# Half of the one-hot gate products of a PEER layer replaced by additions in device memory

## The reference

```python
q = (ht @ w_q).reshape(T, PEER_HEADS, 2, D_HALF)
s1, s2 = einsum(q[:, :, 0], k1), einsum(q[:, :, 1], k2)       # T x 8 x 128 each
v1, i1 = lax.top_k(s1, 16);  v2, i2 = lax.top_k(s2, 16)
sc, flat = lax.top_k(v1[..., :, None] + v2[..., None, :], 16)  # of 256 sums
idx = e1 * 128 + e2;  gate = softmax(sc)
act = gelu(einsum('td,thkd->thk', x, u_tab[idx]))
out = einsum('thk,thkd->td', gate * act, v_tab[idx])
```

## Time and profile before

| | |
|---|---|
| median of 3 runs (lowest to highest) | 1903.39 us (1902.47 to 1903.56) |
| the profiled execution's own time | 1903.38 us |
| span of its instructions | 1901.6 us |
| granted TensorE clock, mean | 0.99 |
| up stages (tiles, scores, scatter) | 200 to 600 us and 1113 to 1512 us |
| down stages | 601 to 975 us and 1514 to 1890 us |

### The profile page before, as it was taken

The page is one execution under the profiler, slowest core; times in us unless marked ns, Lnnn a source line. Parts: engine busy times, 40 slices in busy tenths (PEclk is TensorE's granted clock), DMA queues, the critical chain, the costliest instruction groups (busy, mean ns, idle before and its releaser), DMA issues.

```text
span 1901.6 us, 39850 instructions
## 1 busy us (share of the span) xinstructions
PE 1860.2 (98%) x14863; PEld 1726.2 (91%) x14863; DVE 1524.4 (80%) x2634; ACT 858.2 (45%) x1281; POOL 4.0 (0%) x8
## 2 busy tenths in 40 slices
PE   5999999999999999999999999999999999999998
PEld 5999999999999888888889999999999988888887
DVE  7986689888888888888868768889788888885555
ACT  3335444454434444455444544444434444445453
POOL 0000000000000000000000000000000000000000
PEclk9999999999999999999988999999999999999999
DMA  7976455555444555688834745555544455555552
GB/s 301 335 277 236 154 179 185 177 176 170 153 166 139 171 176 167 235 325 319 321 127 168 262 158 177 179 185 185 168 146 165 138 172 165 176 187 190 197 189 99
DMA packets 101344, 370.46 MB, mean 195 GB/s; under 512 B 11168, under 2 KB 11552, under 8 KB 100640
## 3 DMA queue, kind: packets, MB, share of 16 engines
q1 hardware_dynamic: 100848, 367.43, 55.5%
q10 hardware_dynamic: 432, 2.23, 0.3%
HBM read 366.47 MB, written 3.15 MB: 194 GB/s over the span
## 4 chain that ended last, share of the span: by engine, by line
PE 91%; DVE 5%; DMA 2%; issue 1%; ACT 1%; SPq 0%; DVEq 0%; ACTq 0%
PE ps L1156 46%; PE acc L1315 36%; PE gp L1267 5%; DVE acts L591 2%; DVE low L572 2%; PE ps L1135 1%; PE gp L1077 1%; DMA raw<-conv_in 1%; PE gp L1256 1%; DMA acts<-w_mod 1%; PE gp L1099 0%; ACT high L371 0%; DMA raw<-conv_out 0%; PE acc L1094 0%; DVE acts L952 0%
## 5 line engine op out<-in xcount | busy, mean ns | idle before, releaser
L572 DVE TENSOR_TENSOR low<-raw,high 128x1024 fp32r<-128x1024 f32 x596 | 727.7, 1222 | 320.6 <-ACT high L371 318.5
L371 ACT ACTIVATE high<-raw 128x1024 fp32r<-128x1024 f32 x593 | 626.7, 1057 | 483.0 <-PE acc L1315 383.3
L1156 PE MATMUL ps<-mov_h,high 128*128 128x256 f32 x2656 | 761.2, 287 | 9.9 <-DVE mov_l L680 5.4
L1156 PE MATMUL ps<-mov_l,high 128*128 128x256 f32 x2656 | 755.4, 284 | 0.0
L1156 PE MATMUL ps<-mov_h,low 128*128 128x256 f32 x2656 | 755.2, 284 | 0.0
L1156 PEld LDWEIGHTS ps<-mov_h,high 128*128 128x128 f32 x2656 | 513.4, 193 | 11.5 <-issue 8.2
L1156 PEld LDWEIGHTS ps<-mov_l,high 128*128 128x128 f32 x2656 | 513.7, 193 | 0.0
L1156 PEld LDWEIGHTS ps<-mov_h,low 128*128 128x128 f32 x2656 | 513.6, 193 | 0.0
L1315 PE MATMUL acc<-high,mov_h 128*128 128x512 f32 x1024 | 402.6, 393 | 1.0 <-DVE mov_l L1009 0.8
L1315 PE MATMUL acc<-high,mov_l 128*128 128x512 f32 x1024 | 399.0, 390 | 0.0
L1315 PE MATMUL acc<-low,mov_h 128*128 128x512 f32 x1024 | 398.6, 389 | 0.0
(11 more groups left out here) (116 smaller groups left out, 802.4 us busy)
## 6 DMA issues: line engine op xcount, KB each, us to landing
raw<-up SPq DMA_DIRECT2D x256, 512.0 KB, 3.2
raw<-down SPq DMA_DIRECT2D x256, 512.0 KB, 4.0
acts<-w_mod SPq DMA_DIRECT2D x84, 512.0 KB, 5.8
raw<-query SPq DMA_DIRECT2D x32, 512.0 KB, 3.9
raw<-conv_in SPq DMA_DIRECT2D x24, 512.0 KB, 6.8
acts<-w_mod SPq DMA_DIRECT2D x6, 1024.0 KB, 14.7
raw<-conv_out SPq DMA_DIRECT2D x8, 512.0 KB, 7.0
raw<-pool_in SPq DMA_DIRECT2D x8, 512.0 KB, 3.9
```

The lines of the kernel that those rows point to most:

```text
L371: nc.scalar.activation(flat(high[s]), tile_row(s), ACT.Copy).then_inc(high_ready, 1)
L572: nc.vector.tensor_tensor(flat(low[n % RING]), tile_row(n % RING), flat(high[n % RING]).bitcast(F32), ALU.subtract).then_inc(low_ready, 1)
L1156: ins = nc.tensor.matmul(dst, w[s][:, c], m[:, mv], start=(first and n == 0), stop=(last and n == 2), skip_group_check=skip)
```

## The change

Tokens 0 to 127 get their dense gates in another way; tokens 128 to 255 keep the one-hot products, so that a half of the tiles now has 16 sets (pairs behind every sixth `up` tile from tile 83, and behind every eighth of the first 64 `down` tiles).

- A table of 128 x 128 x 128 float32 in device memory for each layer (8.4 MB) is cleared by SP with 16 transfers of 512 KB: layer 0's beside the query tiles and the first 8 `up` tiles of layer 0, layer 1's beside `up` tiles 8 to 39 of layer 0. Their source is `hot2`, filled with zeros.
- In each of the 8 rounds of `retrieval` DVE now finishes the round: softmax, expert number and place in the table (`DEST`). ACT's Exp comes 8 times in a layer, each followed by a load of the Gelu table.
- GpSimd's `add_gates` issues 16 indirect transfers for a round, each of which adds 128 single numbers (one for each token) to the table. A round's transfers wait until those of the round before have landed.
- GpSimd's `fetch` reads the table back, two tiles' gates of 128 tokens at a time (128 KB), into a ring of four buffers. The first is `added`, the other three are places 4 to 7 of `mov_h`, which are free once PE has done the last `up` tile. DVE's `weigh_first` multiplies tiles 2q and 2q + 1 of `A` by them, and ACT's `weight` waits for it.
- PE turns three blocks in place of six, behind tile 79 in place of tile 77.

```diff
-SETS = HALF // 2
-SET = T // SETS
+SET = 8
+SETS = P // SET
+CHUNK = 1024
+CHUNKS = KEYS * P // CHUNK
+WRING = 4
+WTILES = 2
+GROUPS = KEYS // WTILES
...
+        wt = [added[:]] + [mov_h[:, RING + n].bitcast(F32) for n in range(WRING - 1)]
...
+            def clear(layer, at):
+                cols = bass.ds(at, CHUNK) if not isinstance(at, int) else slice(at, at + CHUNK)
+                sp.dma_start(rows[layer][:, cols], nothing).then_inc(zeroed[layer], 16)
...
+            def add_gates(layer, p):
+                pool.wait_ge(picked, layer * HEADS + p + 1)
+                if layer or p:
+                    pool.wait_ge(landed, 16 * TOPK * (layer * HEADS + p))
+                for k in range(TOPK):
+                    col = p * TOPK + k
+                    nc.gpsimd.indirect_dma_start(
+                        table[layer], bass.IndirectOffsetOnAxis(ap=DEST[:, col:col + 1], axis=0),
+                        GT0[:, col:col + 1], None, compute_op=ALU.add).then_inc(landed, 16)
+            def fetch(layer, i, s, free):
+                if free is not None:
+                    pool.wait_ge(weighed, free)
...
+                nc.gpsimd.dma_start(wt[s], rows[layer][:, cols]).then_inc(wt_in[s], 16)
+            for layer in range(LAYERS):
+                pool.wait_ge(zeroed[layer], 16 * CHUNKS)
+                for p in range(HEADS):
+                    add_gates(layer, p)
+                pool.wait_ge(landed, 16 * TOPK * HEADS * (layer + 1))
+                for s in range(WRING):
+                    if s == 1:
+                        pool.wait_ge(product, AT[layer, "down"] + RING)
+                    fetch(layer, 0, s, layer * GROUPS - WRING + s + 1 if layer else None)
...
-                gelus(8, (TURN - RING - 8) // RING)
-                for s in range(RING):
-                    if s == 2:
-                        act.wait_ge(soft_in, layer + 1)
-                        nc.scalar.activation(SC, SC, ACT.Exp).then_inc(soft_exp, 1)
+                exps = {(HEADS + 1) * p + 11: p for p in range(HEADS)}
+                for j in range(8, TURN + 2 * HEADS):
+                    if j in exps:
...
+                        nc.scalar.activation(sc, sc, ACT.Exp).then_inc(soft_exp, 1)
                         load_table(ACT.Gelu)
...
+                    act.wait_ge(weighed, group + (layer * GROUPS + 1))
...
-                a = a[:, :, k * SET:(k + 1) * SET]
+                a = a[:, :, P + k * SET:P + (k + 1) * SET]
...
+            def weigh_first(layer, q):
+                dve.wait_ge(wt_in[q % WRING], 16 * (layer * (GROUPS // WRING) + q // WRING + 1))
+                a = A[:, WTILES * q * T:WTILES * (q + 1) * T].rearrange("p (g t) -> p g t", t=T)[:, :, 0:P]
+                nc.vector.tensor_tensor(a, a, wt[q % WRING].rearrange("p (g t) -> p g t", t=P),
+                                        ALU.mult).then_inc(weighed, 1)
...
-                    if (j - FIRST_SET) % 3 == 2:
+                    if (j - FIRST_SET) % 6 == 4:
                         two_sets(0, k)
                         k += 2
+                weigh_first(layer, 0)
...
                 for g in range(AHEAD):
+                    if g == WTILES:
+                        weigh_first(layer, 1)
                     low_weight(g)
...
-                    if j % 4 == 2:
-                        two_sets(1, j // 4 * 2)
+                    if j + 2 < GROUPS:
+                        weigh_first(layer, j + 2)
+                    if j % 8 == 2:
+                        two_sets(1, j // 8 * 2)
...
-                        if s % 3 == 1:
-                            scatter(0, i, s // 3 * 2, 8)
-                            scatter(0, i, s // 3 * 2 + 1, 8)
+                        if s % 6 == 3:
+                            scatter(0, i, s // 6 * 2, 4)
+                            scatter(0, i, s // 6 * 2 + 1, 4)
```

More of the change, by code:

```diff
@@ L169, in program @@
         EX = part(o + 1088, 2 * T)
-        GT = part(o + 1600, T)
+        GT1 = part(o + 1600, P)
+        PLACE = part(o + 1600 + P, TOPK)
         SUM = part(o + 1856, ROWS)
         RS = part(o + 1872, ROWS)
-        twice = hot2[:, 0, 0]
+        twice = part(15616, KEYS).bitcast(BF16).rearrange("p (n two) -> p n two", two=2)
+        nothing = hot2[:].rearrange("p a b c d -> p (a b c d)").bitcast(F32)
+        own = part(15616 + KEYS, P)
         v16 = part(o + 1888, 4 * TOPK).rearrange("p (r s n) -> p r s n", r=2, s=2)
@@ L214, in program @@
         soft_in, soft_exp = sem("soft_in"), sem("soft_exp")
+        picked, landed, weighed = sem("picked"), sem("landed"), sem("weighed")
+        zeroed = [sem(f"zeroed{n}") for n in range(LAYERS)]
+        wt_in = [sem(f"wt_in{n}") for n in range(WRING)]
         pick_done, turned, turned_out = sem("pick_done"), sem("turned"), sem("turned_out")
@@ L316, in _ @@
                                      ).then_inc(gate2_in[k], 16)
-                run(layer, "up", KEYS)
+                    elif layer == 0:
+                        clear(0, j // 2 * CHUNK)
+                if layer == 0:
+                    for j in range(8):
+                        load(0, "up", j, j % RING)
+                        clear(0, (8 + j) * CHUNK)
+                    with sp.Fori(0, CHUNKS // 2) as i:
+                        for s in range(RING):
+                            load(0, "up", i * RING + (8 + s), s)
+                            if s % 2:
+                                clear(1, i * (2 * CHUNK) + s // 2 * CHUNK)
+                    run(0, "up", KEYS - 8 - CHUNKS // 2 * RING, 8 + CHUNKS // 2 * RING)
+                else:
+                    run(1, "up", KEYS)
                 run(layer, "down", HALF)
@@ L361, in _ @@
             nc.gpsimd.memset(macc[:, 2:MODS].rearrange("p m n -> p (m n)"), 0.0).then_inc(const_ready, 1)
+            nc.gpsimd.memset(nothing, 0.0).then_inc(const_ready, 1)
+            def add_gates(layer, p):
[10 more added lines that the diff above has]
+                    pool.wait_ge(weighed, free)
+                n = WTILES * P
+                at = i * (WRING * n) + s * n
+                cols = bass.ds(at, n) if not isinstance(at, int) else slice(at, at + n)
+                nc.gpsimd.dma_start(wt[s], rows[layer][:, cols]).then_inc(wt_in[s], 16)
[8 more added lines that the diff above has]
+                    fetch(layer, 0, s, layer * GROUPS - WRING + s + 1 if layer else None)
+                with pool.Fori(0, GROUPS // WRING - 1) as i:
+                    for s in range(WRING):
+                        fetch(layer, i + 1, s, i * WRING + (layer * GROUPS + s + 1))
         @block.scalar
@@ L828, in retrieval @@
                     found = did(ins)
+                    need(top)
+                    need(found)
+                    sc = turn(SC, TOPK)[:, 2 * p:2 * p + 2]
+                    nc.vector.tensor_tensor(sc, sc, RS[:, 2 * p:2 * p + 2].unsqueeze(2).broadcast_to([P, 2, TOPK]),
+                                            ALU.subtract).then_inc(soft_in, 1)
+                    for _ in before:
+                        pass
                     beside()
-                    need(found)
                     before = numbers(p)
[L833 to L838, removed]
                 for _ in before:
                     beside()
[L841 to L847, removed]
+                dve.wait_ge(picked, HEADS * (layer + 1))
+                dve.sem_inc(pick_done, 1)
+                while tile[0] < FIRST_SET:
                     beside()
                 dve.wait_ge(turned, layer + 1)
-                nc.vector.tensor_copy(idx1[:], gp[:, 0, 0:T]).then_inc(turned_out, 1)
-                nc.vector.tensor_copy(idx2[:], gp[:, 0, T:2 * T]).then_inc(turned_out, 1)
-                full = gp[:, 1, 0:T].rearrange("p (h two) -> p h two", two=2)
+                if layer == 0:
+                    for n in range(LAYERS):
+                        dve.wait_ge(zeroed[n], 16 * CHUNKS)
+                nc.vector.tensor_copy(idx1[:], gp[:, 0, 0:P]).then_inc(turned_out, 1)
+                nc.vector.tensor_copy(idx2[:], gp[:, 0, P:2 * P]).then_inc(turned_out, 1)
+                full = gp[:, 1, 0:P].rearrange("p (h two) -> p h two", two=2)
                 rest = gate_rest.rearrange("p (h two) -> p h two", two=2)
@@ L1319, in down_banks, with arrived, down_tile @@
                         return ins
[L1321 to L1327, removed]
+                    def arrived(i, s, per=RING):
+                        pe.wait_ge(low_ready, i * per + (n0 + half * HALF + s + 1))
+                        pe.wait_ge(wl_ready, i * per + (layer * KEYS + half * HALF + s + 1))
+                    def down_tile(i, s, per=RING):
+                        arrived(i, s, per)
+                        down_banks(s % RING, range(4), False).then_inc(product, 1)
                     if half == 0:
-                        with pe.Fori(0, HALF // RING) as i:
-                            for s in range(RING):
-                                down_tile(i, s)
```

(3 more changed lines are left out.)

86 lines of the change are left out of this document (57 added, 29 removed).

## The result

| | before | changed |
|---|---|---|
| median of 4 runs (lowest to highest) | 1902.93 us (1902.19 to 1903.56) | 1853.05 us (1850.83 to 1854.15) |
| the profiled execution, own time | 1903.38 us | 1854.15 us |
| span | 1901.6 us | 1852.5 us |

The ratio is 0.9737 (95% interval 0.972 to 0.9753). The change takes off 49.9 us; I had forecast 44.9. The direction was right and PE's time went where I had said; the largest term of the sum, what a pair of sets costs, was too small.

The account below looks back on a forecast made before the run. PE, busy 98% of the span, was taken as the bound, with the sets' products hidden under nothing: 1903.4 - 47.0 - 0.7 + 2.8 = 1858.5 us. Likeliest case 1854 to 1871 us; range of 8 in 10, 1853 to 1896 us.

Parts of the forecast that it names:

- the products (47.0 us): PE, up and down stages: 32 of 64 pairs of one-hot sets go at 1.47 us each, 47.0 us less.
- Taken away: The PE work that goes: half of the 3072 one-hot products, 47.0 us, and three transposes a layer, 0.7 us.
- a pair's price is not what goes away: Sign that the forecast is wrong: removing a pair of sets does not save its 1.47 us.
- The transposes (0.7 us): PE: three of six transposes go in each layer, 2 x 0.33 = 0.7 us less.
- DVE: Second half of up, first of down: 155 us busy in 187 us; beside the picking about 1.6 us more a round; price nothing.
- the fall to 10: Beside the picking, DVE's wait for `high` was to fall from 26 us to 10 or so.
- GpSimd: Additions to the table during up: 1.7 us for one indirect transfer, limit 2.4 us, price nothing below that.
- the last addition near tile 85: Sign in the up stage: GpSimd's last addition is issued near tile 85 at 1.7 us each, well before the last tile.
- The rival: GpSimd too slow, end of up: over 2.4 us a transfer the first fetch is late; 1884 to 2038 us; chance 0.13.
- DVE held up by GpSimd: Rival beside the picking: transfers hold DVE, 0.33 us each ending at about 1903 us, 1 us each about 2070; chance 0.12.
- Clears (0 to 6 us): SP's 32 transfers of 512 KB, tight beside the query tiles at 158 to 181 us: 0 taken, 6 us upper bound.
- The passage (2.8 us): From up to down: PE waits 1.4 us a layer for the second set behind a fetch landing, 2.8 us; bounds 0 to 9.

Follow-up runs that it names:

- the bench: Changed kernel plus five stretches of 16 indirect transfers behind its end, DVE idle or busy: 1.55 us a transfer with DVE idle, 2.21 beside long subtractions.
- the two benches: Changed kernel with measurements behind its end: transfers beside DVE's operations (1.55 to 2.21 us each), and transfers of fewer places with DVE idle (112 places more cost 0.25 us).
- my first attempt: Changed kernel with the first two one-hot sets of down made ahead of both waits for fetched gates: 1860.24 us, ratio 0.9785.

## Where the prediction failed, and what of it held

**The step that failed: the products (47.0 us).** It is the first term of "Taken away", 32 x 1.47. Right in kind: 32 pairs are gone, and the chain had charged 1.47 us for each. The term was too small, because I took a pair's price from its own stretch of the chain. The tile behind it pays too. From the spacings before and after, a pair costs 20.35 - 18.81 = 1.54 us in up (two periods of 10.175 us before, one of 18.81 after) and 24.96 - 23.35 = 1.61 us in down: 16 x 1.54 + 16 x 1.61 = 50.4 us. The 3.4 us between are most of the 5.0 us that I missed; leaving all products out gave 1.52 to 1.60 us a pair. The rows to see it were there: the four tiles behind the transposes took 11.50 us, the three between pairs 8.70, which is 2.88 against 2.90 us a tile. My sign "a pair's price is not what goes away" came true by 5 to 10%.

**The transposes (0.7 us).** The profile has 435.98 to 436.31 us for three: 0.33 us a layer, as worked out.

**DVE.** In the half of down with sets it is busy 149 of 178 us, 0.84 of the time, where 155 of 187 (0.83) was forecast. Beside the picking its wait for `high` fell from 26.5 to 18.8 us, less than the fall to 10 that I named: the small instructions added 4.5 us in 229 to 430 us (174.5 to 179.0 us busy), 0.6 us a round and not 1.6. PE never waited. ACT's eight Exps did not show on PE either.

**GpSimd.** I took 1.7 us for one, between 0.33 and 3.1, and a limit of 2.4. It was 2.18 with the gap, so the step held, but the cover is thin: 17 and 8 us of 330 a layer. I expected the last addition near tile 85, and that did not follow from my own numbers: a round of 16 x 1.7 + 3.1 us takes 30.3 us, the picking only 25.9, so GpSimd falls behind, and 258 + 128 x 1.7 + 7 x 3.1 us is 497 us, about tile 99. It comes at 566 us, at about tile 121. The 1.88 us are 1.55 us of its own and 0.33 of waiting; the bench shows that DVE's long two-input operations can add up to 0.66, and how much of the 0.33 is theirs was not separated. The rival was closer than 0.13 says: two transfers more a round cost 26 to 28 us.

**DVE held up by GpSimd.** Did not happen: its operations keep their lengths beside the transfers, and it is GpSimd that is held.

**Clears (0 to 6 us).** Nothing: PE busy 23.00 of 23 us at 372 GB/s, and up's tile 8 starts at 228.6 us, 0.6 us earlier than before. That is not shown to be a gain of the change: it starts at 228.9 to 229.5 us in the three profiles of the old code and at 226.1 to 229.5 us in the five of the new (without the two benches). A clear took 6.7 us to land.

**The passage (2.8 us).** 1.1 and 1.5 us, 2.6 in all. The landing was 3.35 and 3.73 us; and making the sets ahead of the wait took the loss away.

**Sum.** 47.0 + 3.4 + 0.7 - 2.6 is 48.5 us, and 0.6 us less ahead of up makes 49.1; the spans differ by 49.1. The medians differ by 0.8 us more, which is within the 3.3 us that the runs of the changed kernel spread. The two longer ones (1854.15 and 1853.92 us) have a mean granted clock of 0.990, the two shorter (1850.83 and 1852.18 us) 0.993; what sets it is open.

## What to carry to other kernels

Price interleaved work by the period of the whole pattern, with and without it, and not by its own stretch in the chain: the tiles behind it may pay a toll (here 0.07 to 0.14 us a pair, 5 to 9% of the price). When work moves to an idle engine, count its time per instruction against the whole window, and look at the lead that is left at the end; "hidden" said nothing here of how near the limit was. When a wait must stay, put behind it only what needs it, and check that what you move in front is not ahead of a shorter chain, as my first attempt was.

## What the runs showed of the hardware that I had not expected

- GpSimd's indirect transfer: 1.55 us for 128 places, 1.29 us for 16, then 0.30 us to the next; a direct fetch of 128 KB took GpSimd 0.54 us.
- It is lengthened to 2.21 us beside back-to-back 128x1024 two-input operations of DVE and to 1.88 us beside multiplications by a constant (then it starts with each second or third of them), but not beside reductions or 128x256 two-input operations; DVE keeps its lengths.
- A group of short products between the tile products costs PE a toll on the tile behind: for bf16 products of 64 columns 0.07 us among products of 256 columns and 0.14 us among those of 512, the same for 16 products as for 48; for float32 products of one column 0.11 us among those of 256; behind float32 products of 128 columns none.
